# VectorE takes over GpSimd's element-wise work in the chunked DeltaNet stage of a decoder layer

## The chip, the cores and the metric

The kernel runs on one core of a Trainium2 chip. The metric is the time on the device of one launch of the whole layer, in microseconds; the time before is the median of three runs.

## The reference, cut to what matters

One inference step of a decoder layer for a prompt of 2048 tokens and 8 sample tokens. Half of the layer's mixing is a gated DeltaNet with 4 heads of width 128. For the prompt it is computed in chunks of tokens; per chunk and head:

```python
gc = cumsum(g)
decay = exp(where(incl, gc[:, None] - gc[None, :], -inf))
kb = k * beta
lower = where(strict, (kb @ k.T) * decay, 0)
a_mat = lower + eye
u = solve(a_mat, v * beta)
w = solve(a_mat, kb * exp(gc))
intra = where(incl, (q @ k.T) * decay, 0)
q_dec, k_dec = q * exp(gc), k * exp(gc[-1] - gc)
v_new = u - w @ state
o = q_dec @ state + intra @ v_new
state = state * exp(gc[-1]) + k_dec.T @ v_new
...
o = rmsnorm(o, g_dn_out) * silu(z)
```

The other half is sliding-window attention under three dilations, of the same prompt. Its scores, softmax and sums stand in the same stage of the kernel.

## The kernel before, in words

The layer is a row of stages, each with its own programs for the five engines; the change is inside one of them, `delta_and_attention`. It runs over 16 chunks of 128 tokens (`NC`), with all 4 heads side by side in tiles of 128 partitions x 512 columns. Every engine has a program written out by hand, in a fixed order, and engines wait for one another by semaphores. A loop of TensorE takes two chunks per turn (seven turns, then two chunks written out); VectorE's loop also takes two, GpSimd's one.

Into each chunk 14 attention steps are woven, called slots 0 to 13 on every engine. In a slot VectorE adds the bias to a pair of score tiles (`s`, L1133), takes the row maximum (L1137) and, in some slots, copies finished sums out (L1143). ScalarE then takes the exponential (L843), TensorE transposes it (L960), ScalarE copies it (L835), and TensorE multiplies it by the values (L972). TensorE computes scores two slots at a time (L945) and may not start the next pair before VectorE has read the last one (`biased`).

Of the DeltaNet work of a chunk, in VectorE's order:

- Start: reciprocals of the norms (L1163, L1165), scaled keys `kn` (L1167) and queries `qn` (L1169) from PSUM, slot 0, the differences of the decays `gd` (L1172), `vb` (L1174), slots 1 and 2. TensorE in the meantime runs slot 0, the decay rows from `gbc` (L998), transposes of raw values (L1002), slot 1 with the turn of slot 0's exponentials (L960), and the transposes of `kn` and `qn` (L1007, L1010).
- Middle: the lower triangle `L` (L1180, L1184), `M` (L1185), `intra` (L1187), `qdec` (L1190), the first inverse `XTh`, `X` (L1193, L1194), slot 3, `intra` again (L1197).
- Six levels of the inverse, each with a slot: TensorE multiplies the masked tile `B[level]` by `XTh` (L919), ScalarE copies `Z` (L863), TensorE multiplies again, and VectorE subtracts into `XTh` (L1202) and `X` (L1216). Between them stand reciprocals for the preceding chunk's output norm (L1148); level 5 ends with that chunk's normalised output (`finish`, L1155). Level 6 writes the last quarter of `XT` (L1208), for which TensorE waits before it can form `W` and `U` (L1058, L1061).
- End: slots 10 to 13, `vnew` (L1220) and the state (L1224, L1226).

GpSimd does eleven products per chunk beside this, all from SBUF: `gbc` (L770, the decays spread over 512 columns, from a tile of ones), `kbg` and `kdec` (L773, L774, from `kn`), six masks of `L` into `B` (L777, 256 columns each), `L21` (L780, 256 columns), and the gating `o * zg` of the preceding chunk (L767, in `finish`). It waits for `kn`, for `L`, for `M` and for the normalised output. SyncE stores the gated output when `out_done` says so (L704), and loads the next gates `zg` behind that (L682).

Of the kernel before, what the change touches and what calls it, by code (L numbers as in the profile page):

```python
# [23 lines left out]
ALU = mybir.AluOpType  # L24
# [3 lines left out]
P = 128  # L28
# [7 lines left out]
HEADS, DK = 4, 128  # L36
# [466 lines left out]
NC = S // CH  # L503
LEVELS = 7
C_IDENT, C_TRIU, C_TRIL, FULL_TILES = 0, 1, 2, 3
HALF_CH = CH // 2
IN_HALF = LEVELS - 1
# [27 lines left out]
def heads(tile):  # L535
    return tile.rearrange("p (h j) -> p h j", h=HEADS)


def per_head(col):

    return col.rearrange("p (h o) -> p h o", o=1).broadcast_to([P, HEADS, P])


def all_heads(tile):

    return tile.rearrange("p (o j) -> p o j", o=1).broadcast_to([P, HEADS, P])


def all_heads_half(tile):

    return tile.rearrange("p (o j) -> p o j", o=1).broadcast_to([P, HEADS, HALF_CH])


def delta_and_attention(nc, t):
# [13 lines left out]
    with ExitStack() as ctx:  # L568
# [8 lines left out]
        beta = sbuf("pb_beta", [P, NC, HEADS], F32)  # L577
        g = sbuf("pb_g", [P, NC, HEADS], F32)
# [3 lines left out]
        ekd = sbuf("pb_ekd", [P, NC, HEADS], F32)  # L582
        raw = sbuf("pb_raw", [P, 12, P], F32)
        zg = sbuf("pb_z", [P, C4], F32)
        squares = sbuf("pb_squares", [P, 8, P], F32)
        ones = sbuf("pb_one", [P, P], F32)
# [3 lines left out]
        betag = sbuf("pb_betag", [P, NC, HEADS], F32)  # L590
        kn, kbg, kdec, qn, vb, knT, qnT, gbc, gd, E, egr, XT, U, WT, vnew, S_, intra, qdec, osq, orr, o, o_raw = (
            sbuf("pb_" + n, [P, C4], F32) for n in
            "kn kbg kdec qn vb knT qnT gbc gd E egr XT U WT vnew S intra qdec osq orr o o_raw".split())
        L, L21, M, X, XTh_, Y, Z = (sbuf("pb_" + n, [P, H4], F32) for n in "L L21 M X XTh Y Z".split())
        B = sbuf("pb_B", [P, IN_HALF, H4], F32)
# [36 lines left out]
        def half_tile(level):  # L632
            first = FULL_TILES * P + (level + 1) * HALF_CH
            return const[:, first:first + HALF_CH]

        def bank(n):
            return ps[:, n, :]
# [6 lines left out]
        def in_half(tile):  # L644
            return tile.rearrange("p (h j) -> p h j", h=HEADS)
# [96 lines left out]
        @block.gpsimd  # L742
        def _(pool):
            pool.memset(ones_mean[:, :], 1.0 / DK).then_inc(consts_set, 1)
            pool.memset(eps[:, :], EPS).then_inc(consts_set, 1)
            pool.memset(S_[:, :], 0.0).then_inc(consts_set, 1)
            pool.memset(XT[:, :], 0.0).then_inc(consts_set, 1)
            pool.memset(ones[:, :], 1.0).then_inc(consts_set, 1)
            for v in range(2):
                pool.memset(qkv[v][:, 1, 4 * P:8 * P], 0.0).then_inc(consts_set, 1)  # L750
                pool.memset(vtok[v][:, 1, :], 0.0).then_inc(consts_set, 1)
                pool.memset(bias[v][:, 0, :].rearrange("p (h k) -> p h k", h=AH)[:, :, 0:P], -BIG).then_inc(consts_set, 1)
            pool.wait_ge(consts_set, 11)
            pool.wait_ge(const_loaded, 80)
            pool.wait_ge(gcol_done, 1)
            def cc(tile, c):

                return tile[:, bass.ds(c, 1), :].rearrange("p o h -> p (o h)")

            def beta_of(c):  # L760
                return cc(beta, c).rearrange("p (h o) -> p h o", o=1).broadcast_to([P, HEADS, HALF_CH])

            def finish(c):

                pool.wait_ge(o1_done, c + 1)
                pool.wait_ge(z_loaded, c * 16 + 16)
                pool.tensor_tensor(o[:, :], o[:, :], zg[:, :], ALU.mult).then_inc(out_done, 1)  # L767

            def chunk(c, first=False):
                pool.tensor_tensor(heads(gbc[:, :]), all_heads(ones[:, :]), per_head(cc(g, c)), ALU.mult).then_inc(gbc_done, 1)  # L770
                pool.wait_ge(k_scaled, c + 1)
                pool.wait_ge(s_upd, c + 1)
                pool.tensor_tensor(heads(kbg[:, :]), heads(kn[:, :]), per_head(cc(betag, c)), ALU.mult)  # L773
                pool.tensor_tensor(heads(kdec[:, :]), heads(kn[:, :]), per_head(cc(ekd, c)), ALU.mult).then_inc(k_side_done, 1)  # L774
                pool.wait_ge(l_done, c + 1)
                for level in range(IN_HALF):
                    pool.tensor_tensor(in_half(B[:, level, :]), in_half(L[:, :]), all_heads_half(half_tile(level)),  # L777
                                       ALU.mult).then_inc(mask_done, 1)
                pool.wait_ge(m_done, c + 1)
                pool.tensor_tensor(in_half(L21[:, :]), in_half(M[:, :]), beta_of(c), ALU.mult).then_inc(mask_done, 1)  # L780
                if not first:
                    finish(c - 1)

            pool.wait_ge(gcol_done, 3)
            pool.wait_ge(betag_done, 1)
            chunk(0, True)
            with pool.Fori(1, NC) as c:
                chunk(c)
            finish(NC - 1)

        @block.scalar
        def _(act):
# [305 lines left out]
        def _(dve):  # L1098
# [51 lines left out]
            def finish(c):  # L1150

                dve.wait_ge(orr_done, c * HEADS + HEADS)
                dve.wait_ge(o_kept, c + 2)
                dve.wait_ge(o_free, c + 1)
                dve.scalar_tensor_tensor(o[:, :], o_raw[:, :], gain[:, 0:1], orr[:, :], ALU.mult, ALU.mult).then_inc(o1_done, 1)  # L1155

            def chunk(c, par, jj, first=False):
                def cc(tile):

                    return tile[:, bass.ds(c, 1), :].rearrange("p o h -> p (o h)")  # L1160

                dve.wait_ge(roots_done, c + 1)
                dve.reciprocal(rr[:, :], rr[:, :]).then_inc(coef_steps, 1)  # L1163
                dve.wait_ge(coef_steps, c * 2 + 1)
                dve.tensor_scalar(coef[:, :], rr[:, 4:8], DK ** -0.5, None, ALU.mult).then_inc(coef_steps, 1)  # L1165
                dve.wait_ge(kq_raw_turned, 2 * c + 2)
                dve.tensor_tensor(heads(kn[:, :]), heads(bank(0)), per_head(rr[:, 0:4]), ALU.mult).then_inc(k_scaled, 1)  # L1167
                dve.wait_ge(coef_steps, c * 2 + 2)
                dve.tensor_tensor(heads(qn[:, :]), heads(bank(1)), per_head(coef[:, :]), ALU.mult).then_inc(q_scaled, 1)  # L1169
                slot(c, par, jj, 0)  # L1170
# [12 lines left out]
                beta_half = cc(beta).rearrange("p (h o) -> p h o", o=1).broadcast_to([P, HEADS, HALF_CH])  # L1183
                dve.tensor_tensor(in_half(L[:, :]), in_half(L[:, :]), beta_half, ALU.mult).then_inc(l_done, 1)  # L1184
                dve.tensor_tensor(in_half(M[:, :]), heads(bank(3))[:, :, TOP], heads(E[:, :])[:, :, TOP], ALU.mult).then_inc(m_done, 1)  # L1185
                dve.wait_ge(scores_done, c + 1)
                dve.tensor_tensor(intra[:, :], bank(2), E[:, :], ALU.mult).then_inc(i1_done, 1)  # L1187
                dve.wait_ge(egr_done, c + 1)
                dve.wait_ge(qnT_copied, c + 1)
                dve.tensor_tensor(qdec[:, :], qnT[:, :], egr[:, :], ALU.mult).then_inc(qdec_done, 1)  # L1190
                dve.wait_ge(b0_turned, c + 1)
                ident4 = all_heads_half(half_tile(-1))
                dve.tensor_tensor(in_half(XTh), ident4, in_half(half_bank(0)), ALU.subtract).then_inc(xt_sub, 1)  # L1193
                dve.tensor_tensor(in_half(X[:, :]), ident4, in_half(B[:, 0, :]), ALU.subtract).then_inc(x_sub, 1)  # L1194
                slot(c, par, jj, 3)
                dve.wait_ge(i1_done, c + 1)
                dve.tensor_tensor(heads(intra[:, :]), heads(intra[:, :]), all_heads(const_tile(C_TRIU)), ALU.mult).then_inc(intra_done, 1)  # L1197
                for level in range(1, LEVELS):
                    slot(c, par, jj, level + 3)
                    dve.wait_ge(xt_done, c * (LEVELS - 1) + level)  # L1200
                    if level < IN_HALF - 1:
                        m = dve.tensor_tensor(XTh, XTh, half_bank(1), ALU.subtract)  # L1202
                    elif level < IN_HALF:
                        for half in (BOTTOM, TOP):
                            m = dve.tensor_tensor(heads(XT[:, :])[half, :, half], in_half(XTh)[half], in_half(half_bank(1))[half],
                                                  ALU.subtract)
                    else:
                        m = dve.tensor_scalar(heads(XT[:, :])[TOP, :, BOTTOM], in_half(half_bank(1))[TOP], -1.0, None, ALU.mult)  # L1208
                    m.then_inc(xt_sub, 1)
                    if level <= HEADS and not first:  # L1210
                        invert(c - 1, level - 1)
                    if level == HEADS + 1 and not first:
                        finish(c - 1)
                    if level < IN_HALF:
                        dve.wait_ge(x_done, c * (LEVELS - 2) + level)
                        dve.tensor_tensor(X[:, :], X[:, :], half_bank(2), ALU.subtract).then_inc(x_sub, 1)  # L1216
# [18 lines left out]
            for h in range(HEADS):  # L1235
                invert(NC - 1, h)
            finish(NC - 1)


QB = S // P  # L1240
# [2111 lines left out]
```

## Time and profile before

| What | Value |
|---|---|
| Median of 3 runs | 3599.97 us (3597.28 to 3603.94) |
| Profiled execution: its time, its span | 3607.1 us, 3605.3 us |
| Chunk stage, first to last start of L1163 | 823.9 to 1579.0 us |
| PE, VectorE, ScalarE, GpSimd busy, whole span | 91%, 63%, 41%, 40% |
| Mean granted TensorE clock | 0.960 |

Times of rows count from the span's start. A row of the time line gives start, duration, engine, line, operation, what is written and read, and in square brackets how long the engine was idle before it and what ended that. VectorE's instructions overlap a little in the records: what one costs the next is read from start to start.

### The profile page before, as it was taken

The page shows a single profiled execution, that of the slowest core. Times are in us where ns is not written, and L with a number is a line of the kernel's source. Part 1 is how long each engine was busy: PE and PEld are TensorE (multiplying, and loading weights), DVE is VectorE, ACT ScalarE, POOL GpSimd, SP SyncE. Part 2 cuts the span into 40 slices and gives each one's busy share as a digit, 9 for nine tenths or more (in the row PEclk, how much of TensorE's full clock was granted, in tenths as well). Part 3 has the DMA queues.
Part 4 walks back from the last instruction along what each step waited for, and adds up shares of the span by engine and source line. Part 5 has one row for each costly group of instructions (what it writes and reads, how often), then busy time and mean ns, then how long its engine had stood idle before and what let it go on. Part 6 is the DMA issues. An engine that isn't in the chain of part 4 may idle for free. (4 is left out here: it accounts for less than half of the span.)

```text
span 3605.3 us, 64498 instructions
## 1 busy us (share of the span) xinstructions
PE 3291.6 (91%) x25026; PEld 3113.0 (86%) x25026; DVE 2265.3 (63%) x2861; ACT 1476.1 (41%) x3047; POOL 1442.2 (40%) x868
## 2 busy tenths in 40 slices
PE   8999999877888888885987999999999899999997
PEld 7899999746777777774986999999999899999997
DVE  6554122255666666676867999999988444334665
ACT  5111122226665666662334454454444343433332
POOL 3111111001112221224314988988887345454232
PEclk9999999968999999996998999999999999999998
DMA  3223244474333333326343553654433455565221
GB/s 118 72 77 77 95 165 165 146 212 129 99 83 89 97 90 95 91 63 188 115 134 129 191 191 117 207 183 142 162 109 109 142 183 183 168 211 186 92 80 70
DMA packets 304824, 473.54 MB, mean 131 GB/s; under 512 B 62830, under 2 KB 250414, under 8 KB 287232
## 3 DMA queue, kind: packets, MB, share of 16 engines
q1 hardware_dynamic: 304584, 470.21, 41.5%
q8 instruction: 166, 2.72, 0.3%
q14 instruction: 74, 0.61, 0.1%
HBM read 342.08 MB, written 161.50 MB: 140 GB/s over the span
## 5 line engine op out<-in xcount | busy, mean ns | idle before, releaser
L78 PE MATMUL gu_ps<-gu_xhi,gu_whi 128*128 128x344 f32 x1848 | 598.8, 324 | 18.2 <-DVE gu_xlo L2530 13.4
L80 PE MATMUL gu_ps<-gu_xlo,gu_whi 128*128 128x344 f32 x1848 | 594.4, 322 | 0.0
L79 PE MATMUL gu_ps<-gu_xhi,gu_wlo 128*128 128x344 f32 x1848 | 590.9, 320 | 0.0
L2371 POOL TENSOR_TENSOR gu_wlo<-gu_wsum,gu_whi 128x512 fp32r<-128x512 f32 x264 | 418.3, 1597 | 96.4 <-ACT gu_whi L2397 96.3
L78 PE MATMUL pa_proj<-pa_h_hi,pa_whi 128*128 128x412 f32 x1160 | 408.3, 352 | 24.9 <-DVE pa_h_lo L409 16.5
L79 PE MATMUL pa_proj<-pa_h_hi,pa_wlo 128*128 128x412 f32 x1160 | 408.1, 352 | 0.0
L80 PE MATMUL pa_proj<-pa_h_lo,pa_whi 128*128 128x412 f32 x1160 | 406.9, 351 | 0.0
L78 PEld LDWEIGHTS gu_ps<-gu_xhi,gu_whi 128*128 128x128 f32 x1848 | 349.5, 189 | 22.9 <-DVE gu_xlo L2530 12.4
L2874 POOL TENSOR_TENSOR pe_wlo<-down_w,pe_whi 128x1408 fp32r<-128x1408 f32 x76 | 256.5, 3387 | 253.1 <-ACT pe_whi L2909 253.1
L79 PEld LDWEIGHTS gu_ps<-gu_xhi,gu_wlo 128*128 128x128 f32 x1848 | 350.1, 189 | 0.4
L80 PEld LDWEIGHTS gu_ps<-gu_xlo,gu_whi 128*128 128x128 f32 x1848 | 349.2, 189 | 0.0
L2371 POOL TENSOR_TENSOR gu_wlo<-gu_w,gu_whi 128x512 fp32r<-128x512 f32 x198 | 319.7, 1622 | 68.1 <-ACT gu_whi L2397 68.1
L78 PE MATMUL pe_prod<-pe_ahi,pe_whi 128*128 128x412 f32 x880 | 311.2, 354 | 17.2 <-DVE pe_alo L3122 9.0
L79 PE MATMUL pe_prod<-pe_ahi,pe_wlo 128*128 128x412 f32 x880 | 308.9, 351 | 0.0
L80 PE MATMUL pe_prod<-pe_alo,pe_whi 128*128 128x412 f32 x880 | 308.8, 351 | 0.0
L252 POOL TENSOR_TENSOR pa_wlo<-pa_w,pa_whi 128x1024 fp32r<-128x1024 f32 x29 | 85.8, 2959 | 514.2 <-ACT pa_whi L277 514.2
L2397 ACT ACTIVATE gu_whi<-gu_wsum 128x512 fp32r<-128x512 f32 x264 | 165.2, 626 | 298.4 <-DVE gu_wsum L2540 137.5
L3129 DVE TENSOR_TENSOR pe_acc<-pe_acc,pe_sq 128x412 f32<-128x412 f32 x35 | 68.0, 1942 | 296.8 <-ACT pe_sq L2932 296.7
L78 PEld LDWEIGHTS pa_proj<-pa_h_hi,pa_whi 128*128 128x128 f32 x1160 | 219.5, 189 | 27.8 <-issue 26.3
L472 DVE TENSOR_TENSOR pa_work<-pa_proj,pa_rstd 128x412 f32<-128x412 f32 (+1 forms) x85 | 49.7, 586 | 298.2 <-PE pa_proj L80 296.3
L2909 ACT ACTIVATE pe_whi<-down_w 128x1408 fp32r<-128x1408 f32 x80 | 110.0, 1381 | 273.5 <-DMA down_w<-in_w_down 253.3
L79 PEld LDWEIGHTS pa_proj<-pa_h_hi,pa_wlo 128*128 128x128 f32 x1160 | 219.2, 189 | 1.9 <-issue 0.8
(394 smaller groups left out, 7622.5 us busy)
## 6 DMA issues: line engine op xcount, KB each, us to landing
gu_w<-in_w_gate_up SPq DMA_DIRECT2D x66, 1024.0 KB, 5.6
down_w<-in_w_down SPq DMA_DIRECT2D x78, 704.0 KB, 4.1
scratch_at<-pa_work SPq DMA_DIRECT2D x24, 1024.0 KB, 5.6
pb_qkv<-scratch_at SPq DMA_DIRECT2D x32, 768.0 KB, 6.6
scratch_a<-gu_row SPq DMA_DIRECT2D x110, 172.0 KB, 5.7
out_new_cache_k<-in_cache_k SPq DMA_DIRECT2D x8, 2046.0 KB, 11.7
out_new_cache_v<-in_cache_v SPq DMA_DIRECT2D x8, 2046.0 KB, 11.4
pa_w<-in_w_in SPq DMA_DIRECT2D x29, 512.0 KB, 5.7
```

The lines of the kernel that those rows point to most:

```text
L78: pe.matmul(out, w_hi, a_hi, start=first, stop=False)
L79: pe.matmul(out, w_lo, a_hi, start=False, stop=False)
L80: return pe.matmul(out, w_hi, a_lo, start=False, stop=last)
L252: pool.tensor_tensor(w_lo[:, par, :], w_raw[:, par, :], w_hi[:, par, :].bitcast(F32), ALU.subtract).then_inc(w_lo_done, 1)
L472: dve.tensor_tensor(into[0:parts, block_cols(b)], ps[0:parts, b, 0:TB], rstd[0:parts, block_cols(b)], ALU.mult).then_inc(evacuated, 1)
L2371: pool.tensor_tensor(w_lo[:, i, :], w_piece(W_PIECES[i], par), w_hi[:, i, :].bitcast(F32), ALU.subtract).then_inc(w_lo_done, 1)
L2397: act.activation(w_hi[:, i, :], w_piece(part, par), ACT.Copy).then_inc(w_hi_done, 1)
L2874: pool.tensor_tensor(w_lo[:, q, :], w_raw[:, q % 2, :], w_hi[:, q, :].bitcast(F32), ALU.subtract).then_inc(w_lo_done, 1)
L2909: act.activation(w_hi[:, q, :], w_raw[:, half, :], ACT.Copy).then_inc(w_hi_done, 1)
L3129: dve.tensor_tensor(acc[:, :], acc[:, :], sq[:, j % 2, :], ALU.add).then_inc(sums_done, 1)
```

## The change

GpSimd keeps only its memsets in this stage. Its eleven products per chunk move into VectorE's program, at these places: `gbc` at the very start of a chunk, `kbg` and `kdec` between `kn` and `qn`, mask 0 behind `M`, mask 1 behind `qdec`, mask 2 behind `X`, masks 3, 4 and 5 behind the slots of levels 1, 2 and 3, `L21` behind the slot of level 4, and the gating directly behind `finish`. The waits for values of other engines go with them. The instructions, their sizes and the semaphores that they raise stay the same.

```diff
 pool:
-            def chunk(c, first=False):
-                pool.tensor_tensor(heads(gbc[:, :]), all_heads(ones[:, :]), per_head(cc(g, c)), ALU.mult).then_inc(gbc_done, 1)
...
 dve:
+            def gate_output(c):
+                dve.wait_ge(o1_done, c + 1)
+                dve.wait_ge(z_loaded, c * 16 + 16)
+                dve.tensor_tensor(o[:, :], o[:, :], zg[:, :], ALU.mult).then_inc(out_done, 1)
+
+            def masked(level):
+                dve.tensor_tensor(in_half(B[:, level, :]), in_half(L[:, :]), all_heads_half(half_tile(level)),
+                                  ALU.mult).then_inc(mask_done, 1)
...
             def chunk(c, par, jj, first=False):
+                dve.tensor_tensor(heads(gbc[:, :]), all_heads(ones[:, :]), per_head(cc(g)), ALU.mult).then_inc(gbc_done, 1)
                 dve.wait_ge(roots_done, c + 1)
...
                 dve.tensor_tensor(heads(kn[:, :]), heads(bank(0)), per_head(rr[:, 0:4]), ALU.mult).then_inc(k_scaled, 1)
+                dve.wait_ge(k_scaled, c + 1)
+                dve.tensor_tensor(heads(kbg[:, :]), heads(kn[:, :]), per_head(cc(betag)), ALU.mult)
+                dve.tensor_tensor(heads(kdec[:, :]), heads(kn[:, :]), per_head(cc(ekd)), ALU.mult).then_inc(k_side_done, 1)
                 dve.wait_ge(coef_steps, c * 2 + 2)
                 dve.tensor_tensor(heads(qn[:, :]), heads(bank(1)), per_head(coef[:, :]), ALU.mult).then_inc(q_scaled, 1)
...
+                dve.wait_ge(l_done, c + 1)
+                masked(0)
...
                 dve.tensor_tensor(qdec[:, :], qnT[:, :], egr[:, :], ALU.mult).then_inc(qdec_done, 1)
+                masked(1)
                 dve.wait_ge(b0_turned, c + 1)
+                dve.wait_ge(mask_done, c * LEVELS + 1)
...
+                masked(2)
                 slot(c, par, jj, 3)
...
                 for level in range(1, LEVELS):
                     slot(c, par, jj, level + 3)
+                    if level + 2 < IN_HALF:
+                        masked(level + 2)
+                    if level + 2 == IN_HALF:
+                        dve.wait_ge(m_done, c + 1)
+                        dve.tensor_tensor(in_half(L21[:, :]), in_half(M[:, :]), beta_half, ALU.mult).then_inc(mask_done, 1)
                     dve.wait_ge(xt_done, c * (LEVELS - 1) + level)
...
                     if level == HEADS + 1 and not first:
                         finish(c - 1)
+                        gate_output(c - 1)
```

`IN_HALF` is 6 and `LEVELS` is 7. Behind the last chunk `gate_output(NC - 1)` follows `finish(NC - 1)`.

## Rows read from the trace of the kernel before

**Rows 1.** Windows view, two chunks: busy us (count) of each engine, granted clock, DMA.

```profile
1220.00:1320.00 100.00, 87.62 (x1306) 74.43 (x1306) 66.83 (x123) 61.81 (x195) 20.43 (x22) 0.97 0.34 90
```

**Rows 2.** Lines by form, GpSimd, chunk stage: count, busy us, mean ns, idle before, releaser.

```profile
L777 POOL TENSOR_TENSOR pb_B<-pb_L,pb_const 128x256 f32<-128x256 f32 x96 | 85.5, 923 | 138.0 <-DVE pb_L L1184 138.0
```

**Rows 3.** Time line, VectorE: L1163 opens each chunk; two pairs of chunks.

```profile
1026.45 0.19 DVE L1163 RECIPROCAL pb_rr<-pb_rr 128x8 f32<-128x8 f32 x1
1080.20 0.19 DVE L1163 RECIPROCAL pb_rr<-pb_rr 128x8 f32<-128x8 f32 x1
1128.83 0.19 DVE L1163 RECIPROCAL pb_rr<-pb_rr 128x8 f32<-128x8 f32 x1
1180.41 0.19 DVE L1163 RECIPROCAL pb_rr<-pb_rr 128x8 f32<-128x8 f32 x1
1229.05 0.19 DVE L1163 RECIPROCAL pb_rr<-pb_rr 128x8 f32<-128x8 f32 x1
1281.28 0.19 DVE L1163 RECIPROCAL pb_rr<-pb_rr 128x8 f32<-128x8 f32 x1
```

**Rows 4.** Time line, start of an odd chunk: VectorE, ScalarE, TensorE.

```profile
1282.21 0.68 DVE L1169 TENSOR_TENSOR pb_qn<-pb_ps,pb_coef 128x512 f32<-128x512 f32 x1
1282.81 0.68 DVE L1133 SCALAR_TENSOR_TENSOR pb_s<-pb_ps,pb_bias 128x512 f32<-128x512 f32 x1
1283.52 0.69 DVE L1137 TENSOR_REDUCE pb_uo<-pb_s 128x2 f32<-128x512 f32 x1
1284.24 0.51 ACT L843 ACTIVATE pb_e<-pb_s,pb_uo 128x256 f32<-128x256 f32 x1 [1.10 <-DVE pb_uo L1137]
1285.47 0.65 PE L960 MATMUL pb_ps<-pb_const,pb_e 128*128 128x128 f32 x4 [1.64 <-ACT pb_e L843]
```

**Rows 5.** Time line, start of an even chunk: TensorE and VectorE.

```profile
1230.61 1.11 PE L932 MATMUL pb_ps<-pb_const,pb_qkv 128*128 128x128 f32 x4 [2.21 <-issue]
1231.65 1.79 PEld L945 LDWEIGHTS pb_ps<-pb_qkv 64*128 64x128 f32 x16 [0.33 <-issue]
1233.76 0.69 DVE L1133 SCALAR_TENSOR_TENSOR pb_s<-pb_ps,pb_bias 128x512 f32<-128x512 f32 x1 [3.10 <-PE pb_ps L945]
```

**Rows 6.** Lines by form, VectorE, chunk stage: products of two SBUF tiles.

```profile
L1190 DVE TENSOR_TENSOR pb_qdec<-pb_qnT,pb_egr 128x512 f32<-128x512 f32 x16 | 17.1, 1072 | 0.0
L1184 DVE TENSOR_TENSOR pb_L<-pb_L,pb_beta 128x256 f32<-128x256 f32 x16 | 6.8, 425 | 0.6
```

**Rows 7.** Time line, middle of a chunk: first inverse, slot 3, next scores.

```profile
1244.86 0.41 DVE L1193 TENSOR_TENSOR pb_XTh<-pb_const,pb_ps 128x256 f32<-128x256 f32 x1
1245.19 0.61 DVE L1194 TENSOR_TENSOR pb_X<-pb_const,pb_B 128x256 f32<-128x256 f32 x1
1245.73 0.68 DVE L1133 SCALAR_TENSOR_TENSOR pb_s<-pb_ps,pb_bias 128x512 f32<-128x512 f32 x1
1246.56 0.97 PEld L945 LDWEIGHTS pb_ps<-pb_qkv 64*128 64x128 f32 x16 [0.17 <-DVE pb_s L1133]
```

**Rows 8.** Lines by form and time line: levels of the inverse.

```profile
L1202 DVE TENSOR_TENSOR pb_XTh<-pb_XTh,pb_ps 128x256 f32<-128x256 f32 x64 | 26.8, 418 | 27.6 <-PE pb_ps L919 27.6
...
1253.17 0.68 DVE L1143 COPY pb_uo<-pb_ps 128x512 f32<-128x512 f32 x1
1253.77 0.41 DVE L1202 TENSOR_TENSOR pb_XTh<-pb_XTh,pb_ps 128x256 f32<-128x256 f32 x1
1256.19 0.69 DVE L1133 SCALAR_TENSOR_TENSOR pb_s<-pb_ps,pb_bias 128x512 f32<-128x512 f32 x1 [0.88 <-PE pb_ps L945]
1268.97 1.16 PE L1058 MATMUL pb_ps<-pb_XT,pb_kbg 128*128 128x128 f32 x8 [0.51 <-DVE pb_XT L1208]
```

**Rows 9.** Windows view: stretches at the start and at the end of a chunk.

```profile
1230.20:1236.90 6.70, 6.29 (x34) 5.50 (x35) 2.72 (x5) 3.26 (x7) 2.04 (x2) 0.50 0.12 43
1284.00:1286.00 2.00, 0.53 (x5) 0.54 (x6) 2.00 (x4) 1.76 (x6) 0.50 (x1) 1.00 0.26 69
1066.30:1069.70 3.40, 3.40 (x16) 3.40 (x16) 0.00 (x0) 0.03 (x1) 0.23 (x1) 0.50 0.72 155
```

More of the change, by code:

```diff
@@ L752, in _ @@
                 pool.memset(bias[v][:, 0, :].rearrange("p (h k) -> p h k", h=AH)[:, :, 0:P], -BIG).then_inc(consts_set, 1)
[L753 to L767, printed above, removed]
-            def chunk(c, first=False):
-                pool.tensor_tensor(heads(gbc[:, :]), all_heads(ones[:, :]), per_head(cc(g, c)), ALU.mult).then_inc(gbc_done, 1)
[L771 to L789, printed above, removed]
         @block.scalar
@@ L1237, in _ @@
             finish(NC - 1)
+            gate_output(NC - 1)
 QB = S // P
```

## The prediction

> **What bounds the kernel now.** I looked for the stage first, then for the engine order inside one chunk, because the change touches nothing outside the chunk stage. A window over two chunks shows TensorE busy for 87.6 of 100 us, VectorE for 66.8, ScalarE for 61.8 and GpSimd for 20.4 [rows 1]. No engine is full, so the stage is a chain of hand-overs, and what an instruction costs depends on whether its engine stood idle just behind it. GpSimd's masks waited 138.0 us for VectorE [rows 2]; it was never late itself, so what is taken from it frees no path.
>
> VectorE's first instruction of each chunk gives the chunk times [rows 3]: an odd chunk (1180.41 to 1229.05) takes 48.64 us, the even one behind it 52.23, and the even ones from 1026.45 and from 1128.83 take 53.75 and 51.58. The difference is at the start. TensorE's loop turns there and TensorE stands for 2.21 us, and VectorE then waits 3.10 us for the first scores of an even chunk [rows 5]. In an odd chunk VectorE goes from `qn` to `s` to the maximum without a pause, ScalarE waits 1.10 us for that maximum, and TensorE 1.64 us for ScalarE's exponential [rows 4]: VectorE leads the chain there.
>
> **The price of one instruction on VectorE.** From start to start, 512 columns cost 0.60 us (`qn` to `s`), and 0.71 where the next waits for the result (`s` to its maximum) [rows 4], so such a wait adds 0.11, and I take 0.12. 256 columns cost 0.33 (`XTh` to `X`) [rows 7]. New instructions, per chunk: four of 512 and seven of 256 columns, and two new waits for a result (`kbg` for `kn`, the gating for `o`): 4 x 0.60 + 7 x 0.33 + 2 x 0.12 = 4.95 us.
>
> What goes is GpSimd's interference. `qdec`, of two SBUF tiles, lasts 1.07 us [rows 6], `qn` of the same size 0.68 [rows 4]: 0.39 too long. `X` takes 0.54 to the next start where 0.33 is normal [rows 7]: 0.21. Both run beside GpSimd's masks. Relief: 0.60 per chunk.
>
> **Step by step.**
>
> *Chunk start.* `gbc` (0.60), `kbg` (0.60 and the wait, 0.12) and `kdec` (0.60) come before `qn`, so before slot 0: 1.92 us. Even chunks cover them with VectorE's 3.10 us of idle time; if that cover went, they would cost the same 1.92. In the odd chunks and in chunk 14, which has no loop turn in front of it, everything behind slot 0's maximum moves by 1.92: ScalarE's exponential, TensorE's turn of it, then `kn` and `qn`, which stand behind that turn in TensorE's order. Nine chunks: 17.3 us. TensorE's decay rows stand behind slot 0's scores in its order and should just find `gbc` ready.
>
> *Masks 0 to 2.* Mask 0 on VectorE ends about where GpSimd's ended, one instruction behind `M`. The three add 0.99 in front of slot 3, less the relief of 0.60: 0.39. TensorE's next scores wait for slot 3's `s` [rows 7], so this goes through.
>
> *Masks 3, 4, 5 and `L21`.* They stand in front of the wait of `XTh`. Over four levels that wait is 27.6 us in 64 instructions, 0.43 each [rows 8], which covers 0.33; but not at level 2, where `XTh` starts 0.60 behind the copy, with no wait at all, and where TensorE is so late afterwards that the next `s` waits 0.88 for scores [rows 8]. So mask 4 costs 0.33, the other three together an estimated 0.06. With 0.39 that makes 0.78 a chunk, 12.5 us in 16.
>
> *Gating.* 0.60 and a wait of 0.12 to 0.13 behind `finish`: 0.73, in front of `X`, slot 9, the copy and the last quarter of `XT`, for which TensorE waits 0.51 us [rows 8]. Fifteen chunks: 11.0 us. The gates it waits for were sent for a chunk earlier. SyncE's store gets its signal at nearly the same moment as before (the product starts later and is shorter), so nothing behind it in SyncE's queue moves. At the very end the gating takes 0.73 instead of GpSimd's time for 512 columns, which I bound from below by the 0.92 of half the size [rows 2]: a gain of some 0.5.
>
> *TensorE's clock.* In the even chunk the granted clock was 0.50 from 1230.20 to 1236.90, that is 1.2 instead of 2.4 GHz [rows 9], after TensorE had stood for 2.21 us with little work before it; loading weights for the scores took 1.79 us instead of 0.97 [rows 5, 7]. In an odd chunk TensorE stands for 1.64 us and the clock stays at 1.00 [rows 4, 9]. The change makes that 1.64 + 1.92 = 3.56 us, longer than the pause after which it falls. By this row I expect the fall in the odd chunks too. Its price lies between 0 and 3.35 (a stretch as long as the even one, 6.7 us at half speed, all of it packed). I take 1.8, near half of the shortest low stretch shown, 3.40 us [rows 9], because TensorE has work without a break behind that pause: 9 x 1.8 = 16.2 us.
>
> The Trainium skill's page "TensorE: Matmul & The Clock Gate" (section "HAM oscillation — how this bites in real kernels") says that a loop which makes TensorE wait between its groups of matmuls can start every group cold. By that rule the odd starts pay as above; without it the sum below is 16.2 us less.
>
> The clock also fell once at the end of the inverse, from 1066.30 to 1069.70 [rows 9], in the chunk that took 53.75 instead of 51.58 [rows 3]: 2.17 us. There TensorE does small products with waits between, and the wait for `XT` grows from 0.51 to some 1.2. I take six more such falls in 16 chunks, between none and sixteen (0 to 35 us): 6 x 2.2 = 13.2 us.
>
> **Sum.** 17.3 + 12.5 + 11.0 - 0.5 + 16.2 + 13.2 = 69.7 us. The profiled execution took 3607.1, so 3676.8; the median of the runs is 7.1 lower, 3599.97, so 3669.7. I say 3670.
>
> The page "VectorE: DVE Perf Modes" (section "The DRAIN you can't avoid"; the Trainium skill) has the next operation start only when the pipe is empty. The rows differ: 0.60 from start to start for a record of 0.68 [rows 4], and 0.33 for one of 0.41 [rows 7]; so the measurement decides. By the rule the sum would be some 8 us more (0.08 or 0.09 for each instruction that counts above).
>
> **The rivals.**
>
> *The clock holds.* Only VectorE's extra time counts: 17.3 + 12.5 + 11.0 - 0.5 = 40.3, so 3640. For it: the clock stayed up over 1.64 us. Against it: 2.21 us brought it down.
>
> *VectorE becomes the bound everywhere.* Then nothing of the 4.95 less 0.60 hides, in any chunk: 4.35 x 16 = 69.6, with the two clock terms 99, so 3699. For it: VectorE would be busy for some 76 of 100 us. Against it: the 3.10 us in even chunks and the 0.43 before `XTh`.
>
> *Not slower: the end of the interference decides.* VectorE has 33.2 us idle in 100 [rows 1], some 16 a chunk, against 4.95 of new work. If all of it fell into that, only the relief would show, 0.60 x 16 = 9.6, so 3590. It decides if slot 0's maximum and the last quarter of `XT` are not what TensorE waits for last. Against it: TensorE's 1.64 and 0.51 [rows 4, 8] both lead back to VectorE. The Trainium skill's page "SBUF — State Buffer" (section "SBUF: two separate sides") describes this interference as a lock that VectorE's two-tile products and GpSimd take in turns; the 1.07 us of `qdec` agree.
>
> That the change does not do what it says is out: GpSimd's program has only memsets left.
>
> **How the numbers follow.** The forecast with both clock terms has 0.60, the clock that holds 0.20, VectorE as the bound 0.13, the end of the interference 0.07. The range goes from 3630, the clock rival with a quarter of its 40 hidden, to 3699, the bound. About 0.2% (7 us) is what a measurement of this kernel can tell from no change. Of the last rival's 0.07, 0.04 is faster by more, 0.03 within it; I give 0.02 of the clock rival's chance to no difference as well. So 0.04 faster, 0.05 same, 0.91 slower. The likeliest case's own range, by the bounds of its clock terms, is 3645 to 3699.
>
> **What would show each step right or wrong.** Odd chunks longer by 3.4 us and more, even ones by about 1.5; TensorE's wait for the first exponentials near 3.6 us in odd chunks, followed by a granted clock of 0.50; `qdec` at 0.68; the wait before L1058 at 1.2. If odd chunks grow by less than 1.5, slot 0's maximum was not on the path; if even chunks grow as much as odd ones, the cover at their start is gone; if the clock in odd chunks stays at 1.00, the time should be near 3640.

## The result, and the profile after

The changed kernel takes 3671.57 us (median of 4 runs, 3664.44 to 3681.61) against 3598.62 before: 2.0% longer, ratio 1.0199 with a 95% interval of 1.0173 to 1.0225. The forecast was 3670. The profiled execution took 3673.32 us, its span 3671.3; the span before was 3605.3, so 66.0 us are to be found in the traces. The last instruction of the chunk stage ends at 1696.2 us instead of 1632.6, and the stage begins some 4 us earlier (its first L1136 at 819.8, L1163 before at 823.9), so the stage holds the loss.

In the changed file VectorE's chunk begins with `gbc` at L1134, 0.60 us before the reciprocal (L1163 before, now L1136); L1184 is now L1160. The time line of VectorE, kernel after: the start of a chunk for chunks 8 to 11, and for chunk 9 the products that are new there and the end of its start.

```profile
1255.79 0.20 DVE L1136 RECIPROCAL pb_rr<-pb_rr 128x8 f32<-128x8 f32 x1
...
1307.72 0.68 DVE L1134 TENSOR_TENSOR pb_gbc<-pb_one,pb_g 128x512 f32<-128x512 f32 x1
1308.32 0.20 DVE L1136 RECIPROCAL pb_rr<-pb_rr 128x8 f32<-128x8 f32 x1
1308.64 0.69 DVE L1140 TENSOR_TENSOR pb_kn<-pb_ps,pb_rr 128x512 f32<-128x512 f32 x1
1309.46 0.69 DVE L1142 TENSOR_TENSOR pb_kbg<-pb_kn,pb_betag 128x512 f32<-128x512 f32 x1
1310.07 0.68 DVE L1143 TENSOR_TENSOR pb_kdec<-pb_kn,pb_ekd 128x512 f32<-128x512 f32 x1
1311.27 0.68 DVE L1096 SCALAR_TENSOR_TENSOR pb_s<-pb_ps,pb_bias 128x512 f32<-128x512 f32 x1
1320.87 0.42 DVE L1160 TENSOR_TENSOR pb_L<-pb_L,pb_beta 128x256 f32<-128x256 f32 x1
...
1361.83 0.20 DVE L1136 RECIPROCAL pb_rr<-pb_rr 128x8 f32<-128x8 f32 x1
1416.06 0.20 DVE L1136 RECIPROCAL pb_rr<-pb_rr 128x8 f32<-128x8 f32 x1
```

Even chunk 8 takes 52.53 us, odd chunk 9 53.51, against 52.23 and 48.64 before [rows 3]: the odd ones pay most. From `L` to the next chunk's reciprocal chunk 9 takes 40.96 us. The same stretch before was 38.81 in chunk 8: the first row here (time line, VectorE, kernel before) to the one at 1281.28 in [rows 3].

```profile
1242.47 0.43 DVE L1184 TENSOR_TENSOR pb_L<-pb_L,pb_beta 128x256 f32<-128x256 f32 x1
...
1291.11 0.43 DVE L1184 TENSOR_TENSOR pb_L<-pb_L,pb_beta 128x256 f32<-128x256 f32 x1
```

Of these 2.15 us, 0.60 are the next chunk's `gbc`; the middle grew by 1.55. The start of chunk 9, from its `gbc` to `L`, takes 13.15 us; before, chunk 9's start took 9.83 (1281.28 to the second row), and the other odd ones 9.76 to 9.83.

TensorE in that chunk, time line of the kernel after (L923 is the turn of the first exponentials, L960 before; L1021 the first product with the finished inverse, L1058 before):

```profile
1313.92 1.11 PE L923 MATMUL pb_ps<-pb_const,pb_e 128*128 128x128 f32 x4 [3.66 <-ACT pb_e L806]
1314.83 1.06 PE L970 MATMUL pb_ps<-pb_const,pb_kn 128*128 128x128 f32 x4
...
1348.92 1.16 PE L1021 MATMUL pb_ps<-pb_XT,pb_kbg 128*128 128x128 f32 x8 [1.02 <-DVE pb_XT L1194]
```

The pause is 3.66 us instead of 1.64 [rows 4], and behind it the 4 turns take 1.11 us instead of 0.65. The wait for the last quarter of `XT` is 1.02 instead of 0.51 [rows 8]. The windows view of the kernel after (columns as in [rows 1]) shows the granted clock, for the pause, for what follows it, for a stretch at the end of an inverse, and for 100 us of the stage:

```profile
1310.30:1313.30 3.00, 0.00 (x0) 0.00 (x0) 2.96 (x6) 0.60 (x3) 0.00 (x0) 1.00 0.49 141
1313.30:1316.70 3.40, 2.77 (x14) 2.45 (x14) 1.85 (x3) 3.40 (x11) 0.00 (x0) 0.50 0.39 107
1402.10:1405.50 3.40, 3.40 (x20) 3.18 (x20) 0.00 (x0) 0.57 (x2) 0.00 (x0) 0.50 0.61 155
1200.00:1300.00 100.00, 81.86 (x1268) 69.46 (x1267) 72.45 (x141) 57.18 (x173) 0.00 (x0) 0.98 0.33 85
```

VectorE is busy for 72.5 of 100 us, TensorE for less than before (81.9, against 87.6 in [rows 1]). VectorE's groups, lines by form, kernel after: the masks, level waits, gating and decayed queries.

```profile
L1126 DVE TENSOR_TENSOR pb_B<-pb_L,pb_const 128x256 f32<-128x256 f32 x96 | 39.9, 416 | 0.0
L1188 DVE TENSOR_TENSOR pb_XTh<-pb_XTh,pb_ps 128x256 f32<-128x256 f32 x64 | 26.7, 417 | 15.5 <-PE pb_ps L882 14.7
L1123 DVE TENSOR_TENSOR pb_o<-pb_o,pb_z 128x512 f32<-128x512 f32 x16 | 11.1, 692 | 2.0
L1168 DVE TENSOR_TENSOR pb_qdec<-pb_qnT,pb_egr 128x512 f32<-128x512 f32 x16 | 10.9, 680 | 0.0
```

`qdec` is down from 1.07 [rows 6] to 0.68 us with GpSimd silent, and the idle time before `XTh` fell from 27.6 us [rows 8] to 15.5: masks stand in it now.

### The profile page after: what moved, and what is told of

Its sections match the earlier page's. It is cut to its first block and busy times, and to the rows that moved or that the text cites. A ratio compares the mean times of both kernels' runs of the same rounds, so it can differ in the third digit from the quotient of the medians.

```text
span 3671.3 us, 64432 instructions
## 1 busy us (share of the span) xinstructions
PE 3314.9 (90%) x25026; PEld 3130.9 (85%) x25026; DVE 2336.0 (64%) x3037; ACT 1478.4 (40%) x3047; POOL 1278.9 (35%) x692
## 5 line engine op out<-in xcount | busy, mean ns | idle before, releaser
L78 PEld LDWEIGHTS pa_proj<-pa_h_hi,pa_whi 128*128 128x128 f32 x1160 | 218.8, 189 | 27.6 <-issue 25.5
```

The lines of the kernel that those rows point to most:

```text
L78: pe.matmul(out, w_hi, a_hi, start=first, stop=False)
```

## The experiments

Each run has its own runs of the kernel before beside it (medians 3602.0 to 3602.5 us, where the first comparison had 3598.62; a few us between runs that stand apart are no finding). All but the one with `M` and `qdec` moved start from the changed kernel. The code behind the stage is the same in all, and took 1966.8 to 1975.1 us in the eleven traces, so the steps are read inside the stage. Three explanations were put to them: A, the place of each product on the path, and the clock that falls behind longer pauses; B, VectorE as the bound, where every product counts in full in every chunk; C, the place alone, without the clock.

**The three products of the start on GpSimd again.**

```diff
 dve:
-                dve.tensor_tensor(heads(gbc[:, :]), all_heads(ones[:, :]), per_head(cc(g)), ALU.mult).then_inc(gbc_done, 1)
...
-                dve.tensor_tensor(heads(kbg[:, :]), heads(kn[:, :]), per_head(cc(betag)), ALU.mult)
-                dve.tensor_tensor(heads(kdec[:, :]), heads(kn[:, :]), per_head(cc(ekd)), ALU.mult).then_inc(k_side_done, 1)
 pool:
...
+            def chunk(c):
+                pool.tensor_tensor(heads(gbc[:, :]), all_heads(ones[:, :]), per_head(cc(g, c)), ALU.mult).then_inc(gbc_done, 1)
+                pool.wait_ge(k_scaled, c + 1)
+                pool.wait_ge(s_upd, c + 1)
+                pool.tensor_tensor(heads(kbg[:, :]), heads(kn[:, :]), per_head(cc(betag, c)), ALU.mult)
+                pool.tensor_tensor(heads(kdec[:, :]), heads(kn[:, :]), per_head(cc(ekd, c)), ALU.mult).then_inc(k_side_done, 1)
+                pool.wait_ge(xt_sub, c * LEVELS + LEVELS)
...
```

> The changed kernel with the three products of the chunk start (decay rows, two scaled keys) on GpSimd again; masks and gating stay on VectorE. Theory A (place on the path, and the clock behind the pause): the odd chunks and chunk 14 lose 1.92 us of VectorE's time and about 1.7 of low clock, some 3.6 each, even chunks gain nothing: 9 x 3.6 = 32, so about 3640 us, with the start of odd chunks back at 9.8 us. Theory B (VectorE is the bound, every instruction counts everywhere): 1.92 in each of 16 chunks, 31 us, so about 3641, but spread evenly, odd starts at about 10.9. Theory C (place without clock): 9 x 1.92 = 17, so 3654.

Measured: 3641.24 us, ratio 1.0111 (1.0095 to 1.0128). Time line of VectorE (chunk 9) and TensorE in it:

```profile
1293.68 0.19 DVE L1155 RECIPROCAL pb_rr<-pb_rr 128x8 f32<-128x8 f32 x1
1297.86 0.65 PE L943 MATMUL pb_ps<-pb_const,pb_e 128*128 128x128 f32 x4 [1.64 <-ACT pb_e L826]
1303.51 0.42 DVE L1176 TENSOR_TENSOR pb_L<-pb_L,pb_beta 128x256 f32<-128x256 f32 x1
...
1343.86 0.19 DVE L1155 RECIPROCAL pb_rr<-pb_rr 128x8 f32<-128x8 f32 x1
```

The odd start is 9.83 us, as before the change, the pause 1.64, at full clock; the middle is still long, 40.35. The total could not tell A from B, but the place does: in the traces the odd starts and chunk 14's give back 32.6 us, the even ones of chunks 2 to 12 nothing (0.3 us more). That is more than C's 17, and 3641 lies well under C's 3654. So the clock was part of it.

**TensorE kept busy in its pause, odd chunks.** Nothing of VectorE's program changes.

```diff
 pe:
                 m.then_inc(raw_turned, 1)
+                if par:
+                    pe.wait_ge(q_scaled, c + 1)
+                    for again in range(5):
+                        for h in range(HEADS):
+                            pe.transpose(col(bank(1), h), ident, ident)
                 slot(c, par, 1)
```

> The changed kernel; in odd chunks TensorE fills its pause before the first exponentials with 20 transposes of the identity into a bank that is overwritten next, so that it does not stand still. Nothing else moves. Theory A: the granted clock stays at 1.00 at the start of odd chunks, each loses about 1.7 us, 8 x 1.7 = 13, so about 3658 us. Theories B and C: the clock is not a cost, no change, 3671 us, or a little more if the filler is in the way.

Measured: 3648.39 us, ratio 1.0129 (1.0112 to 1.0146). TensorE in chunk 9, time line, then VectorE's `L` there:

```profile
1305.83 2.40 PE L971 MATMUL pb_ps<-pb_const 128*128 128x128 f32 x20 [1.15 <-DVE pb_qn L1150]
1308.35 0.65 PE L923 MATMUL pb_ps<-pb_const,pb_e 128*128 128x128 f32 x4
...
1313.99 0.43 DVE L1165 TENSOR_TENSOR pb_L<-pb_L,pb_beta 128x256 f32<-128x256 f32 x1
```

With work whose result nobody reads the kernel is 23 us faster. The turns take 0.65 us again and begin as late behind the reciprocal as without the filler (5.62 us in chunk 9, 5.60 in the changed kernel), and no odd start shows a low clock. Over the eight odd starts the trace has 89.9 us instead of 101.9, 12 less, near the 13 expected. The other 11 are not this step's: in the profiled runs about 7 lie behind the stage, and some 5 in the middles, where the clock fell seven times instead of nine. With 11.26 us from reciprocal to `L` the odd start still stands 2.03 over 9.83 once `gbc` is added: VectorE's own part.

**TensorE kept busy at the end of the inverse.**

```diff
 pe:
+                for again in range(2):
+                    for h in range(HEADS):
+                        pe.transpose(col(bank(3), h), ident, ident)
                 pe.wait_ge(xt_sub, c * LEVELS + LEVELS)
```

> The changed kernel; at the end of the inverse TensorE fills its wait for the last quarter with 8 transposes of the identity into a bank that is free there, in every chunk. Theory A: the falls of the granted clock some 40 us into a chunk (nine in the changed kernel's trace, one before) become rare, each fall saved is worth 1.6 to 2.7 us: some 8 x 1.9 = 15, so about 3656 us. Theories B and C: no change, 3671 us.

Measured: 3655.0 us, ratio 1.016 (1.0136 to 1.0184). TensorE at the end of chunk 9's inverse, time line: the filler, and behind it without a wait the first product with the finished inverse.

```profile
1342.45 1.09 PE L1020 MATMUL pb_ps<-pb_const 128*128 128x128 f32 x8
1343.54 1.16 PE L1024 MATMUL pb_ps<-pb_XT,pb_kbg 128*128 128x128 f32 x8
```

None of the 15 middles shows a low clock, and those of chunks 1 to 14 take 40.85 to 41.08 us (the changed kernel: 40.85 to 43.72); together the 15 are 16.1 us shorter, where A had some 15.

**Both fillers.**

> The changed kernel with both fillers of TensorE's waits. VectorE's program is the changed one. Theory A: no low clock in odd starts nor at the end of the inverse; only VectorE's extra time is left, 40.3 us over the kernel before: 3640 us, between 3633 and 3648. If the two savings overlap, 3648 us as with the first filler alone.

Measured: 3643.87 us, ratio 1.0114 (1.0096 to 1.0132). No odd start and no middle shows a low clock. It is left at the start of five of the six even chunks 2 to 12, where it was before the change too, and at that of chunk 14, whose pause has no filler; there the kernel before shows none. Of the 73 us lost, 28 came back without touching VectorE's program.

**Only the gating on GpSimd again.**

```diff
 dve:
                         finish(c - 1)
-                        gate_output(c - 1)
...
 pool:
...
+            def gated(c):
+                pool.wait_ge(o1_done, c + 1)
+                pool.wait_ge(z_loaded, c * 16 + 16)
+                pool.tensor_tensor(o[:, :], o[:, :], zg[:, :], ALU.mult).then_inc(out_done, 1)
...
```

> The changed kernel with only the gating of the output on GpSimd again. Theory A: a chunk from L to the next chunk's first reciprocal, 40.95 us at full clock in the changed kernel, becomes 40.2; TensorE's wait for the last quarter is about 0.5 us again, so that the clock falls there less often: 15 x 0.73 = 11 us and up to 8 falls of 1.8, so 3646 to 3660 us. If the gating was covered (a rival for this step): 40.95 stays and the time is 3671 us.

Measured: 3649.23 us, ratio 1.013 (1.0112 to 1.0149). Chunk 9 from `L` on, and TensorE's wait in it (time line):

```profile
1312.88 0.43 DVE L1177 TENSOR_TENSOR pb_L<-pb_L,pb_beta 128x256 f32<-128x256 f32 x1
1340.19 1.16 PE L1038 MATMUL pb_ps<-pb_XT,pb_kbg 128*128 128x128 f32 x8 [0.51 <-DVE pb_XT L1211]
1353.10 0.20 DVE L1153 RECIPROCAL pb_rr<-pb_rr 128x8 f32<-128x8 f32 x1
```

40.22 us and a wait of 0.51: 0.74 of the gating was on the path, and without it the clock fell at that place in three middles instead of nine (one trace of each).

**Only the masks on GpSimd again.**

```diff
 dve:
...
-                masked(0)
...
-                masked(1)
...
-                masked(2)
...
-                    if level + 2 < IN_HALF:
-                        masked(level + 2)
...
 pool:
...
+            def masks(c):
+                pool.wait_ge(l_done, c + 1)
+                for level in range(IN_HALF):
+                    pool.tensor_tensor(in_half(B[:, level, :]), in_half(L[:, :]), all_heads_half(half_tile(level)),
+                                       ALU.mult).then_inc(mask_done, 1)
...
```

(`L21` goes with them in the same way.)

> The changed kernel with the six masks and the last quarter's mask on GpSimd again. Theory A: from L to the next chunk 40.95 us becomes about 40.2 (0.78 less), and the decayed queries take 1.07 us again beside GpSimd: 16 x 0.78 = 12.5, about 3659 us, with as many falls of the clock. If masks counted in full without the interference (7 x 0.33 = 2.3 a chunk): 38.6 and 3634 us.

Measured: 3659.03 us, ratio 1.0154 (1.0134 to 1.0174). At full clock (chunks 6, 8, 10 and 11) the middle is 40.14 to 40.16 us, 0.80 less than 40.95. Chunk 8's time line, and lines by form of both engines:

```profile
1267.35 0.43 DVE L1182 TENSOR_TENSOR pb_L<-pb_L,pb_beta 128x256 f32<-128x256 f32 x1
1307.51 0.20 DVE L1158 RECIPROCAL pb_rr<-pb_rr 128x8 f32<-128x8 f32 x1
```

```profile
L765 POOL TENSOR_TENSOR pb_B<-pb_L,pb_const 128x256 f32<-128x256 f32 x96 | 85.0, 919 | 752.6 <-DVE pb_L L1182 752.6
L1188 DVE TENSOR_TENSOR pb_qdec<-pb_qnT,pb_egr 128x512 f32<-128x512 f32 x16 | 17.3, 1080 | 0.0
```

The interference is back with the masks, 1.08 us for `qdec`. Seven masks cost 0.80 a chunk net, not 2.3.

**All eleven products on VectorE, in other places.** The decay rows of the next chunk go into the wait before the state, the scaled keys behind slots 1 and 2, the later masks, `M` and `qdec` into the waits of the levels, the gating into the wait before slot 10.

```diff
 dve:
...
                 slot(c, par, jj, 1)
...
+                dve.tensor_tensor(heads(kbg[:, :]), heads(kn[:, :]), per_head(cc(betag)), ALU.mult)
                 slot(c, par, jj, 2)
+                dve.tensor_tensor(heads(kdec[:, :]), heads(kn[:, :]), per_head(cc(ekd)), ALU.mult).then_inc(k_side_done, 1)
...
+                    if level == 1:
+                        masked(2)
+                        masked(3)
+                        dve.tensor_tensor(in_half(M[:, :]), heads(bank(3))[:, :, TOP], heads(E[:, :])[:, :, TOP], ALU.mult).then_inc(m_done, 1)
+                    if level == 3:
+                        masked(4)
+                    if level == 4:
+                        masked(5)
+                    if level == 5:
...
+                        dve.tensor_tensor(in_half(L21[:, :]), in_half(M[:, :]), beta_half, ALU.mult).then_inc(mask_done, 1)
...
+                        dve.tensor_tensor(qdec[:, :], qnT[:, :], egr[:, :], ALU.mult).then_inc(qdec_done, 1)
...
+                if not first:
+                    gate_output(c - 1)
                 slot(c, par, jj, 10)
...
                 slot(c, par, jj, 11)
+                dve.tensor_tensor(heads(gbc[:, :]), all_heads(ones[:, :]),
+                                  per_head(g_ext[:, bass.ds(c + 1, 1), :].rearrange("p o h -> p (o h)")), ALU.mult).then_inc(gbc_done, 1)
```

> All eleven products stay on VectorE, in other places: decay rows of the next chunk in the wait before the state, scaled keys behind slots 1 and 2, masks 2 and 3 (and M) in the wait of level 1, mask 4 in that of level 3, mask 5 of level 4, the last quarter's mask and the decayed queries in that of level 5, gating in the wait before slot 10. VectorE does the same work. Theory A: almost all of it is covered, and the front of the inverse is shorter by about 0.6 us a chunk than in the kernel before: 3590 us, between 3580 and 3605, no longer than before. Theory B: as the changed kernel, 3671 us.

Measured: 3588.46 us, ratio 0.9966 (0.9954 to 0.9979): 0.3% faster than the kernel before, too. A window of 100 us, the waits of the levels, and chunk 9 (windows, lines by form, time line):

```profile
1220.00:1320.00 100.00, 87.74 (x1322) 74.45 (x1322) 75.58 (x146) 62.49 (x196) 0.00 (x0) 0.98 0.38 92
```

```profile
L1195 DVE TENSOR_TENSOR pb_XTh<-pb_XTh,pb_ps 128x256 f32<-128x256 f32 x64 | 26.6, 416 | 1.7 <-PE pb_ps L883 0.9
```

```profile
1269.33 0.19 DVE L1139 RECIPROCAL pb_rr<-pb_rr 128x8 f32<-128x8 f32 x1
1279.16 0.42 DVE L1163 TENSOR_TENSOR pb_L<-pb_L,pb_beta 128x256 f32<-128x256 f32 x1
1317.39 0.19 DVE L1139 RECIPROCAL pb_rr<-pb_rr 128x8 f32<-128x8 f32 x1
```

VectorE is busier than in the changed kernel, 75.6 of 100 us, and the kernel is 83 us faster. Odd starts take 9.83 us, the middle of chunk 9 38.23 (at full clock 38.2 to 38.4 in all but the first), and only 1.7 us of idle time is left before the 64 `XTh`. This ends B.

**The kernel before with `M` and `qdec` moved.** GpSimd keeps its work.

```diff
 dve:
-                dve.tensor_tensor(in_half(M[:, :]), heads(bank(3))[:, :, TOP], heads(E[:, :])[:, :, TOP], ALU.mult).then_inc(m_done, 1)
...
-                dve.tensor_tensor(qdec[:, :], qnT[:, :], egr[:, :], ALU.mult).then_inc(qdec_done, 1)
...
+                    if level == 1:
+                        dve.tensor_tensor(in_half(M[:, :]), heads(bank(3))[:, :, TOP], heads(E[:, :])[:, :, TOP], ALU.mult).then_inc(m_done, 1)
+                    if level == 5:
...
+                        dve.tensor_tensor(qdec[:, :], qnT[:, :], egr[:, :], ALU.mult).then_inc(qdec_done, 1)
```

> The kernel before, with GpSimd's work where it was; only M and the decayed queries move on VectorE, to the waits of levels 1 and 5, as in the reordered kernel. Tells whether the reordered kernel's gain needs the work to leave GpSimd. If the gain is the order alone: 38.25 us from L to the next chunk instead of 38.81, 16 x 0.56 = 9, 3593 us. If GpSimd's masks still hold the path (mask 0 takes 0.71 there instead of 0.42, and its masks still run beside X): a gain of 0.2 to 0.3 a chunk, 3597 us.

Measured: 3591.85 us, ratio 0.9966 (0.9953 to 0.9979). Lines by form, and chunk 7's time line:

```profile
L1193 DVE TENSOR_TENSOR pb_intra<-pb_intra,pb_const 128x512 f32<-128x512 f32 x16 | 12.1, 756 | 0.0
L1190 DVE TENSOR_TENSOR pb_X<-pb_const,pb_B 128x256 f32<-128x256 f32 x16 | 7.1, 446 | 0.0
```

```profile
1181.20 0.42 DVE L1184 TENSOR_TENSOR pb_L<-pb_L,pb_beta 128x256 f32<-128x256 f32 x1
1219.56 0.19 DVE L1163 RECIPROCAL pb_rr<-pb_rr 128x8 f32<-128x8 f32 x1
```

38.36 us: 0.45 of the 0.58 that the reordered kernel gains in an odd chunk (0.50 in an even one) come from moving two instructions that were on VectorE all along. The second case of the expectation, that GpSimd's masks would hold most of it back, did not come: with `qdec` out of their way they cost VectorE little (`X` 0.45 us, where it had 0.61 before and 0.42 with GpSimd silent; `intra` on average 0.76 instead of 0.68). The 15 middles hold 6.8 of the 10.7 us between the medians; the rest is not placed.

**The reordered kernel again, beside that.**

> The reordered kernel once more, on the same chip as the run above, so that the two can be compared directly: 3588 us as before, 0.2 to 0.4% under the kernel before.

Measured: 3588.03 us, ratio 0.9959 (0.9947 to 0.9972). The two intervals overlap; that leaving GpSimd adds something, 0.14 us in an odd chunk and 0.05 in an even one, is read from the traces only, and the totals don't separate it.

## Why the prediction was right

It was right by its mechanism and nearly by its terms. Starts and middles below are sums over VectorE's rows, after minus before, the start taken from `gbc`, the even starts those of chunks 2 to 12, the middles those of chunks 0 to 14.

| Step | Forecast, us | Shown, us |
|---|---|---|
| Odd starts and chunk 14, VectorE and clock | 17.3 + 16.2 | 32.6 |
| Even starts | 0 | -3.9 |
| Masks and gating, per chunk at full clock | 0.78 + 0.73 | 1.55 in the trace; 0.80 and 0.74 alone |
| Masks and gating, all middles | 12.5 + 11.0 | 22.1 |
| Clock at the end of the inverse | 13.2 (six falls more) | 14.7 (eight more) |
| Rest: up to the first chunk, its start, and all behind the last chunk's `L` | -0.5 | 0.6 |
| Total | 69.7 | 66.0 (span; rows rounded), 73.0 (medians) |

That 3670 came within 2 us of the median is in part luck. The price of a cold start and the number of falls were picked from wide bounds, the gain at the even starts was not foreseen, and the traces hold only 66.0 of the 73.0 us: the profiled execution before took 8.5 us more than its median, the one after 1.8. The signs that were named came: the seven odd chunks 1 to 13 took 6.2 us more on average, the six even ones 1.7.

*Chunk start.* The even chunks' 3.10 us of waiting covered the 1.92, as forecast: where the clock stayed up (chunks 8 and 10) the start takes 12.17 and 12.29 us, and with the three products on GpSimd 12.08 and 12.28. The odd ones had no cover. VectorE's own part came out at 2.03 in the run without the clock's fall. What was mis-sized is the wait for `kn`: from `kn` to `kbg` the trace has 0.82 us from start to start, so the wait adds 0.22, not 0.12. The page "VectorE: DVE Perf Modes" (section "The DRAIN you can't avoid", the Trainium skill), which the prediction sets against its rows, also says that a next operation which is not held starts earlier; so the 0.60 us between the starts of records of 0.68 do not contradict it.

*Even starts.* A term that I had at nothing was a gain of 3.9 us. The low stretches there were four of 3.4 us in six turns, where before there were six, two of them of 6.8. In the run with both fillers five of six were of 6.8. Over the other traces the sum of these starts lies between 3.7 us under the kernel before and 1.0 over it, with the three products on either engine, so nothing ties it to the change; what sets the length of a stretch was not tested.

*Masks.* Net 0.80, against 0.78. The traces show its parts, too. Time line, VectorE: chunk 9 after, then chunk 8 before.

```profile
1324.54 0.68 DVE L1096 SCALAR_TENSOR_TENSOR pb_s<-pb_ps,pb_bias 128x512 f32<-128x512 f32 x1
1332.92 0.41 DVE L1188 TENSOR_TENSOR pb_XTh<-pb_XTh,pb_ps 128x256 f32<-128x256 f32 x1
1344.48 0.85 DVE L1191 TENSOR_TENSOR pb_XT<-pb_XTh,pb_ps 64x256 f32<-64x256 f32 x2 [0.95 <-PE pb_ps L882]
1345.26 0.73 DVE L1118 SCALAR_TENSOR_TENSOR pb_o<-pb_o_raw,pb_gain,pb_orr 128x512 f32<-128x512 f32 x1
1346.13 0.69 DVE L1123 TENSOR_TENSOR pb_o<-pb_o,pb_z 128x512 f32<-128x512 f32 x1
```

```profile
1265.27 0.85 DVE L1205 TENSOR_TENSOR pb_XT<-pb_XTh,pb_ps 64x256 f32<-64x256 f32 x2 [0.95 <-PE pb_ps L919]
1266.05 0.73 DVE L1155 SCALAR_TENSOR_TENSOR pb_o<-pb_o_raw,pb_gain,pb_orr 128x512 f32<-128x512 f32 x1
1266.71 0.40 DVE L1216 TENSOR_TENSOR pb_X<-pb_X,pb_ps 128x256 f32<-128x256 f32 x1
```

From `L` to slot 3's `s` it is 3.67 us instead of 3.26 [rows 7], 0.41 against the forecast 0.39. From there to level 2's `XTh` it is 8.38 instead of 8.04 [rows 7, 8], 0.34 against 0.33 for mask 4. From level 2 to `XT` at level 5 it is 11.56 instead of 11.50, the 0.06 of the others.

*Gating.* 0.74, against 0.73. Its wait was mis-sized like that for `kn`: from `finish` to the gating 0.87 us from start to start, where `finish` to `X` had 0.66 before, so 0.21 and not 0.12 to 0.13; the excess did not reach the path. The wait before L1058 was forecast at 1.2 us and is 1.02, with the gating's full price still in the chunk.

*Clock.* Both places were right, and the fillers show it as a cause: the same program of VectorE is 28 us faster when TensorE does not stand still. Over all traces, odd starts with the long pause show a low clock in 31 of 32 cases (chunk 5 with the filler at the end of the inverse is the exception), with the pause of 1.6 us in none of 40, with the filler in none of 16. At the end of the inverse, chunks 1 to 14, it is 33 of 56 with the wait of 1.02 us, 7 of 70 with 0.51, none of 28 with the filler. The price per odd start, 1.8, was close: 12 us over eight starts is 1.5. The rule of the page "TensorE: Matmul & The Clock Gate" (section "HAM oscillation — how this bites in real kernels", the Trainium skill) agrees with these runs: with the long pause 31 of 32 odd starts were at the low clock, without it none.

*Rivals.* The clock that holds, 3640: the run that made it hold at both places took 3643.87. VectorE as the bound, 3699: refuted by the reordered kernel, which gives VectorE all eleven products in 3588 us. Relief alone, 3590: wrong for this order of instructions, but it is about what the reordered kernel reached, so the idle time that this rival counted was there, only not where the change put its work. The equal number is a coincidence: most of that gain came with `M` and `qdec` moved, GpSimd working as before.

## What to carry to other kernels

An engine at 67% has room for more work only in the places where it waits: read each new instruction's place in the time line, and look there for idle time just behind it and for who waits for what comes next. Where a chain already makes TensorE wait, a longer wait is paid twice, once as time and once in the clock of the work behind it. Before moving work between engines, look for instructions that are early for no reason: two of them, put off to a later wait, gave 0.45 us in each chunk here.

## What the runs showed of the hardware that was not expected

A wait of VectorE for its own result had different prices: 0.11 us from `s` to its maximum [rows 4], 0.21 from `finish` to the gating, 0.22 from `kn` to `kbg`. What sets the price is not shown, and a wait is not the only thing that costs it: from `L` to `M`, with no wait between, 0.46 us passed from start to start in both kernels, where 256 columns else took 0.33.

TensorE's granted clock could be held by work that nobody reads. 20 transposes, 2.40 us in a pause of 3.66, did not delay the turns behind them, which took 0.65 us instead of 1.11 in chunk 9, and the odd starts became 1.5 us shorter on average.
